# Head norms of a two-block transformer kernel: row sums on four column quarters, factors on 1024 columns, broadcast by ones products on four row quarters

## The chip, the cores and the metric

The kernel runs on 1 core of one Trainium2 chip. The metric is the device time of one execution in microseconds (us). Five engines work side by side: TensorE (PE in the profile, its weight loads PEld), VectorE (DVE), ScalarE (ACT), GpSimd (POOL) and SyncE (SP, which issues the loads of the weights). They meet at semaphores only.

## The reference, cut to what matters

Two blocks follow each other on 256 tokens of width 1024: one with gated linear attention and a feed-forward part, one that adds a gated delta rule (8 heads of 128) and a banded attention, and again a feed-forward part. The change touches three norms of the delta rule. Each takes, for one token and one head, the sum of 128 squares:

```
q = l2norm(q.reshape(b_, s_, A_HEADS, A_DK)) * (A_DK ** -0.5)
k = l2norm(k.reshape(b_, s_, A_HEADS, A_DK))
...
o = chunk_gated_delta_rule(q, k, v, g, beta)
o = o * lax.rsqrt(jnp.mean(jnp.square(o), axis=-1, keepdims=True) + RMS_EPS)
o = o * norm_w.astype(jnp.float32) * jax.nn.silu(z...)
```

So one norm has 8 heads x 256 tokens = 2048 factors.

## The kernel before

Activations lie feature-major: 128 features on the partitions, tokens along the columns. A head of q, k or the delta output is one tile of 128 x 256; eight heads are 128 x 2048. All weights stream from HBM as halves of 128 x 1024 (`raw`, a ring of six), which ACT rounds into `w_hi` (L969) and DVE turns into the remainder `w_lo` (L1478), both in rings of four. TensorE multiplies a panel of two halves in four **quarters**, two to a half, each of 12 matmuls (L401; three passes hi*hi, hi*lo, lo*hi), into four `panel_banks`. The other four PSUM banks, `work_banks` (MB in the code), belong to the delta rule and the attention.

Each engine's order is written by hand. While the delta rule is worked out, TensorE fills its gaps with quarters of the later projections: `fill(step)` multiplies as many as the table FILL says stand behind that step, and `tend(step)` on ACT and DVE prepares the halves for them. FILL places 5 quarters behind `k_sums` and 5 more behind `q_sums`, one behind each of the products, 6 behind `delta_out` (quarters 42 to 47), 8 behind `delta_sums` (48 to 55) and 4 behind `delta_norm` (56 to 59). Quarters 2h and 2h+1 need half h (`open_half` waits for `parts_ready`, that is for DVE's `w_lo`). In `tend("delta_sums")` halves 25, 26 and 27 are prepared, in `tend("delta_norm")` halves 28 to 31.

The norms. Squares of q and k are made on ACT (L1259). `qk_norm` (L715) multiplies them by an all-ones matrix, four matmuls of 128 x 512 over the four work banks: each bank then holds the sums, repeated on all 128 partitions. ACT takes Ln and Exp(-0.5 x) of all 2048 columns into SBUF (k at L1288 and L1290, q at L1293 and L1298), and DVE multiplies keys (L1841), beta times keys (L1843) and queries (L1846). Key sums come first, the query sums follow when ACT has read the first. Then L757 makes six groups of 8 products in the same work banks, two banks at a time, and DVE reads each (L1859) before its banks are written again. The delta output has the same pattern: sums (L852), Ln and Exp in two halves of 1024 columns (L983, L984, called by `factor`), two multiplications on DVE (L1920).

An older place in the program, the gates of the first block, already uses parts of the array: L511 multiplies 128-row operands into 32 columns of the array at a time, L521 32-row operands on four row groups.

Of the kernel before, what the change touches and what calls it, by code (L numbers as in the profile page):

```python
# [17 lines left out]
ALU = mybir.AluOpType  # L18
ACT = mybir.ActivationFunctionType
AX_X = mybir.AxisListType.X  # L20

P = 128
D = 1024
# [59 lines left out]
CONSTANTS, GLA_CONSTANTS, ALL_CONSTANTS = 9, 15, 55  # L83
# [37 lines left out]
def two_blocks(nc, panels, x, ctx_x, columns, c_rows, w_glr, w_gate, w_beta_a, head_rows, rel_bias, out):  # L121
# [3 lines left out]
    with ExitStack() as ctx:  # L125
# [5 lines left out]
        def S(name):  # L131

            if name not in signals:
                signals[name] = ctx.enter_context(nc.semaphore(name))
            return signals[name]
# [108 lines left out]
        with ExitStack() as scope:  # L244
# [7 lines left out]
            rs2 = vb.rearrange("p a b -> p (a b)")  # L252
# [3 lines left out]
            rsq = tt_.rearrange("p a b -> p (a b)")  # L256
# [50 lines left out]
        def _(pool):  # L307
            made = [0]

            def step(ins):  # L310
                made[0] += 1
                ins.then_inc(S("constants"), 1)
                pool.wait_ge(S("constants"), made[0])
# [31 lines left out]
            step(pool.memset(eps[:, 2:3], 1.0))  # L345
            step(pool.memset(wgp, 0.0))
# [26 lines left out]
            pool.wait_ge(S("qk_normed"), 2)  # L373
            pool.memset(tt_[64:P, :, 0:64], 0.0).then_inc(S("corner_cleared"), 1)
# [3 lines left out]
        def _(pe):  # L378
# [333 lines left out]
            def qk_norm(part):  # L712

                for b in range(4):
                    ins = pe.matmul(MB[:, b, :], ones[:, 0:P], sq3[:, part * 8 + 2 * b:part * 8 + 2 * b + 2, :],  # L715
                                    start=True, stop=True)
                ins.then_inc(S("qk_sums"), 1)
# [25 lines left out]
            qk_norm(1)  # L743
            fill("k_sums")
            pe.wait_ge(S("sums_read"), 1)
            qk_norm(0)
            fill("q_sums")

            pe.wait_ge(S("sums_read"), 2)
            pe.wait_ge(S("kb_ready"), 1)  # L750
            for r, (rhs, tj, ti) in enumerate(((kb, 0, 0), (kb, 1, 1), (kb, 0, 1), (qkv, 0, 0), (qkv, 1, 1), (qkv, 0, 1))):
                if r == 3:
                    pe.wait_ge(S("qk_normed"), 2)
                if r >= 2:
                    pe.wait_ge(S("products_read"), r - 1)
                for h in range(DH):
                    ins = pe.matmul(MB[:, 2 * (r % 2) + h // 4, (h % 4) * P:(h % 4) * P + P],  # L757
                                    qkv[:, 8 + h, tj * P:tj * P + P], rhs[:, h, ti * P:ti * P + P], start=True, stop=True)
                ins.then_inc(S("products"), 1)
                fill(("product", r))  # L760
# [88 lines left out]
            for b in range(4):  # L849
                pe.wait_ge(S("delta_squares"), b + 1)  # L850
                pe.wait_ge(S("delta_scaled"), b + 1)
                ins = pe.matmul(MB[:, b, :], ones[:, 0:P], odq[:, 2 * b:2 * b + 2, :], start=True, stop=True)  # L852
                if b % 2:
                    ins.then_inc(S("delta_norm_sum"), 1)
            fill("delta_sums")
            fill("delta_norm")

            pe.wait_ge(S("delta_factor"), 2)
# [79 lines left out]
        def _(act):  # L938
# [42 lines left out]
            def factor(out_, sums, n, which, name):  # L981

                then(act.activation(out_, sums, ACT.Ln, scale=1.0 / n, bias=eps[:, which:which + 1]))  # L983
                act.activation(out_, out_, ACT.Exp, scale=-0.5).then_inc(S(name), 1)  # L984
# [183 lines left out]
            def flat(v):  # L1168
                return v.rearrange("p a b -> p (a b)")
# [116 lines left out]
            all_banks = MB[:].rearrange("p a b -> p (a b)")  # L1286
            act.wait_ge(S("qk_sums"), 1)
            act.activation(rs2, all_banks, ACT.Ln, bias=eps[:, 0:1]).then_inc(S("sums_read"), 1)  # L1288
            act.wait_ge(S("sums_read"), 1)
            act.activation(rs2, rs2, ACT.Exp, scale=-0.5).then_inc(S("qk_factor"), 1)  # L1290
            tend("k_sums")
            act.wait_ge(S("qk_sums"), 2)
            act.activation(rsq, all_banks, ACT.Ln, bias=eps[:, 0:1]).then_inc(S("sums_read"), 1)  # L1293
# [3 lines left out]
            act.wait_ge(S("sums_read"), 2)  # L1297
            act.activation(rsq, rsq, ACT.Exp, scale=-0.5).then_inc(S("qk_factor"), 1)  # L1298
# [37 lines left out]
            for n in range(2):  # L1336
                act.wait_ge(S("delta_norm_sum"), n + 1)
                factor(rs2[:, D * n:D * n + D], flat(MB[:, 2 * n:2 * n + 2, :]), DDK, 0, "delta_factor")
# [123 lines left out]
        def _(dve):  # L1462
# [376 lines left out]
            dve.wait_ge(S("qk_factor"), 1)  # L1839
            kc = qkv[:, 8:16, :]  # L1840
            dve.tensor_tensor(flat(kc), flat(kc), rs2, ALU.mult).then_inc(S("qk_normed"), 1)  # L1841
            dve.wait_ge(S("qk_normed"), 1)
            dve.tensor_tensor(flat(kb), flat(kb), flat(kc), ALU.mult).then_inc(S("kb_ready"), 1)  # L1843
            tend("k_sums")
            dve.wait_ge(S("qk_factor"), 2)
            dve.scalar_tensor_tensor(flat(qkv[:, 0:8, :]), flat(qkv[:, 0:8, :]), DDK ** -0.5, rsq,  # L1846
# [68 lines left out]
            tend("delta_out")  # L1915
            dve.wait_ge(S("delta_scaled"), 4)
            for n in range(2):
                dve.wait_ge(S("delta_factor"), n + 1)
                o = flat(od[:, 4 * n:4 * n + 4, :])
                dve.tensor_tensor(o, o, rs2[:, D * n:D * n + D], ALU.mult).then_inc(S("delta_gated"), 1)  # L1920
            tend("delta_sums")
# [231 lines left out]
```

## Time and profile before

| | us |
|---|---|
| median of 3 runs | 1060.26 |
| the three runs | 1060.14, 1060.26, 1066.72 |
| profiled execution | 1059.05 |
| its span | 1057.3 |
| mean granted TensorE clock | 0.973 of full |

The profile is of one execution, and its span is 1.75 us shorter than that execution's time. A record of a matmul in fp32 comes twice (two records for one instruction of the program). Records of matmuls overlap, since they are pipelined: the spacing of their starts, not their length, is what one costs.

### The profile page before, as it was taken

Reading aid. Unit: us, or ns where it says so; the run is one execution under the profiler, and the core shown is the slowest. Engines: PE = TensorE matmul, PEld = TensorE weight load, DVE = VectorE, ACT = ScalarE, POOL = GpSimd, SP = SyncE. Lnnn points to the kernel's source line nnn. Section 1 sums busy time; section 2 is a strip of 40 time slices with the busy share of each in tenths; the row PEclk is TensorE's granted clock in tenths of the full one; section 3 lists DMA queues with packets and bytes.
Section 4 is the critical chain, followed back from the end, with each engine's and each line's share of the span. In section 5 each row is a group of like instructions: output and inputs, shape, how many; then the busy total and the mean of one; then the engine's idle time right before and its main releaser. Section 6 shows DMA issues by size and latency. Waiting matters only on the chain.

```text
span 1057.3 us, 19933 instructions
## 1 busy us (share of the span) xinstructions
PE 980.9 (93%) x8478; PEld 918.5 (87%) x8478; DVE 703.9 (67%) x1098; ACT 551.0 (52%) x830; POOL 27.2 (3%) x70
## 2 busy tenths in 40 slices
PE   5897999979999999699999999989999699999996
PEld 1477999869999999599898999888898699999995
DVE  2669937547777766598865543555668578888743
ACT  2658431555544443565745342656764466666433
POOL 2010000000000000130100000000000000000000
PEclk9898999999999999899999999999999989999999
DMA  9632765536888888247433436444357525555931
GB/s 329 234 121 80 264 234 187 181 127 212 278 275 283 281 274 309 72 149 252 153 120 102 149 113 169 140 160 132 110 201 228 208 99 184 189 188 188 331 100 40
DMA packets 57113, 196.79 MB, mean 186 GB/s; under 512 B 6064, under 2 KB 10560, under 8 KB 56768
## 3 DMA queue, kind: packets, MB, share of 16 engines
q1 hardware_dynamic: 51552, 187.72, 52.3%
q10 hardware_dynamic: 5216, 7.53, 2.6%
q8 instruction: 67, 1.10, 0.4%
q0 software_dynamic: 256, 0.26, 0.1%
q14 instruction: 22, 0.18, 0.0%
HBM read 194.43 MB, written 1.06 MB: 185 GB/s over the span
## 4 chain that ended last, share of the span: by engine, by line
PE 81%; DVE 9%; ACT 5%; DMA 3%; issue 1%; SPq 0%; ACTq 0%; DVEq 0%
PE panel_banks L401 67%; DMA raw<-in_panels 3%; PE work_banks L786 2%; DVE w_lo L1478 2%; PE work_banks L614 2%; ACT w_hi L969 1%; PE work_banks L573 1%; DVE raw L1511 1%; PE work_banks L715 1%; PE panel_banks L454 1%; PE work_banks L757 1%; PE work_banks L546 1%; PE work_banks L869 1%; PE work_banks L488 1%; PE work_banks L814 1%
## 5 line engine op out<-in xcount | busy, mean ns | idle before, releaser
L401 PE MATMUL panel_banks<-act_hi,w_hi 128*128 128x256 f32 (+1 forms) x1600 | 463.3, 290 | 26.3 <-DVE act_lo L1674 11.4
L401 PE MATMUL panel_banks<-act_lo,w_hi 128*128 128x256 f32 (+1 forms) x1600 | 454.5, 284 | 0.0
L401 PE MATMUL panel_banks<-act_hi,w_lo 128*128 128x256 f32 (+1 forms) x1600 | 453.9, 284 | 0.0
L1478 DVE TENSOR_TENSOR w_lo<-raw,w_hi 128x1024 fp32r<-128x1024 f32 x260 | 315.3, 1222 | 163.5 <-ACT w_hi L969 162.8
L969 ACT ACTIVATE w_hi<-raw 128x1024 fp32r<-128x1024 f32 x260 | 272.0, 1054 | 151.4 <-PE panel_banks L401 130.4
L401 PEld LDWEIGHTS panel_banks<-act_hi,w_hi 128*128 128x128 f32 x1600 | 304.6, 190 | 39.5 <-issue 19.5
L401 PEld LDWEIGHTS panel_banks<-act_lo,w_hi 128*128 128x128 f32 x1600 | 304.7, 190 | 1.8 <-issue 0.5
L401 PEld LDWEIGHTS panel_banks<-act_hi,w_lo 128*128 128x128 f32 x1600 | 304.4, 190 | 1.4
L401 PE MATMUL panel_banks<-hidden_hi,w_hi 128*128 128x256 f32 x352 | 98.0, 278 | 2.3 <-ACT hidden_hi L1186 2.3
L401 PE MATMUL panel_banks<-hidden_hi,w_lo 128*128 128x256 f32 x352 | 97.9, 278 | 0.0
L401 PE MATMUL panel_banks<-hidden_lo,w_hi 128*128 128x256 f32 x352 | 97.7, 278 | 0.0
L1511 DVE CUSTOM_DVE_ANT_0 raw<-raw,c_wide 128x1024 f32<-128x1024 f32 x80 | 94.5, 1220 | 0.4 <-DMA raw<-in_panels 0.3
L401 PEld LDWEIGHTS panel_banks<-hidden_hi,w_hi 128*128 128x128 f32 x352 | 65.9, 187 | 2.9 <-ACT hidden_hi L1186 1.7
L401 PEld LDWEIGHTS panel_banks<-hidden_lo,w_hi 128*128 128x128 f32 x352 | 66.1, 188 | 0.0
L401 PEld LDWEIGHTS panel_banks<-hidden_hi,w_lo 128*128 128x128 f32 x352 | 66.1, 188 | 0.0
L401 PE MATMUL panel_banks<-w_hi,act_hi 128*128 128x256 f32 x192 | 54.5, 284 | 2.2 <-DVE w_lo L1478 2.2
L401 PE MATMUL panel_banks<-w_lo,act_hi 128*128 128x256 f32 x192 | 53.4, 278 | 0.0
L401 PE MATMUL panel_banks<-w_hi,act_lo 128*128 128x256 f32 x192 | 53.4, 278 | 0.0
L2053 DVE SCALAR_TENSOR_TENSOR ffn_work<-panel_banks,columns,ffn_work 128x255 f32<-128x255 f32 (+1 forms) x88 | 38.4, 478 | 21.2 <-ACT ffn_work L1434 20.4
L614 PE MATMUL work_banks<-ffn_work,ones 128*128 128x256 f32 x112 | 31.1, 425 | 14.4 <-ACT ffn_work L1412 4.8
L614 PEld LDWEIGHTS work_banks<-ffn_work,ones 128*128 128x128 f32 x112 | 22.3, 210 | 21.1 <-issue 6.2
L1434 ACT ACTIVATE ffn_work<-panel_banks,columns 128x256 f32<-128x256 f32 x44 | 22.4, 561 | 31.4 <-PE panel_banks L401 31.4
(269 smaller groups left out, 1032.9 us busy)
## 6 DMA issues: line engine op xcount, KB each, us to landing
raw<-in_panels SPq DMA_DIRECT2D x356, 512.0 KB, 5.0
mix_work<-delta_rows ACTq DMA_DIRECT2D x2, 1024.0 KB, 11.8
x_t<-in_x ACTq DMA_DIRECT2D x1, 1024.0 KB, 9.4
gla_work<-in_ctx_x ACTq DMA_DIRECT2D x1, 1024.0 KB, 14.3
mix_work<-in_rel_bias ACTq DMA_DIRECT2D x1, 1024.0 KB, 10.0
out_x<-ffn_work SPq DMA_DIRECT2D x2, 512.0 KB, 2.6
mix_work<-in_rel_bias ACTq DMA_DIRECT2D x1, 768.0 KB, 14.3
c_wide<-in_c_rows ACTq DMA_DIRECT2D x1, 512.0 KB, 16.6
```

The lines of the kernel that those rows point to most:

```text
L401: ins = pe.matmul(out_, a, b, start=start and p == 0, stop=stop and p == 2, skip_group_check=True)
L454: ins = pe.matmul(PB[0:2, a % TURNS, 0:256], cact[:, 0:2, 4 * h + k], raw[:, u % RAW, k * 256:k * 256 + 256], start=(h == 0 and k == 0), s ...
L488: ins = pe.matmul(MB[:, 0, :], ones[:, 0:P], sq1[:, k, :], start=(k == 0), stop=(k == 3))
L546: ins = pe.matmul(MB[:, h, t * T:t * T + T], g_k3[:, 4 * d + h, t * P:t * P + P], g_q3[:, 4 * d + h, :], start=(d == 0), stop=(d == 1))
L573: ins = pe.matmul(MB[:, (h + 2) % 4, v * T:v * T + T], g_v[:, n, h * GDV + v * P:h * GDV + v * P + P], g_a[:, h, n, :], start=(n == 2 and ...
L614: ins = pe.matmul(MB[:, bank, 0:T], ones[:, 0:P], src[:, k, :], start=(k == 0), stop=(k == KT - 1))
L786: ins = pe.matmul(o, lhs[half, m, :], rhs[half, m, :], start=True, stop=True)
L969: act.activation(whi[:, v_ % PARTS, :], raw[:, u % RAW, :], ACT.Copy)\
L1434: ins = act.activation(f_u[:, i % 2, m, :], b[:, m * T:m * T + T], ACT.Identity, scale=col("conv_ffn_2", 88 + 22 * m + i), bias=col("b_con ...
L1478: dve.tensor_tensor(wlo[:, v_ % PARTS, :], raw[:, u % RAW, :], whi[:, v_ % PARTS, :].bitcast(F32), ALU.subtract)\
L1511: dve.tensor_tensor_reduce(raw[:, u % RAW, :], raw[:, u % RAW, :], cwide[:], 1.0, 0.0, ALU.mult, ALU.add, dst).then_inc(S("accumulated"), 1)
L2053: ins = dve.scalar_tensor_tensor(o, b[:, m * T:m * T + T - s], col("conv_ffn_2", 44 * (2 - s) + 22 * m + i), o, ALU.mult, ALU.add)
```

## The change

The ones products are cut into pieces that lie side by side in the array. `group_sums` multiplies the squares of two heads per group by 128 x 32 ones; the four groups write the four partition quarters (32 rows each) of one work bank, so that a bank holds all 2048 sums, each repeated on 32 rows. Keys and queries are summed together, into two banks. ACT takes Ln and Exp of 1024 columns once for both, and of 512 columns for the delta output. `spread` brings the factors back to 128 partitions: 32-row ones times 32-row factors, one row quarter to one work bank, 8 matmuls of 256 columns. The sum over 32 equal rows makes a factor 32, which the scale of 1024 under the root takes out (a fourth column of `eps`, one more memset of 128 x 1 at the start). DVE now multiplies by the work banks instead of by SBUF. On TensorE the spread of the keys stands ahead of `fill("q_sums")`, that of the queries behind it, that of the delta output between `fill("delta_sums")` and `fill("delta_norm")`.

```diff
-            def qk_norm(part):
-                for b in range(4):
-                    ins = pe.matmul(MB[:, b, :], ones[:, 0:P], sq3[:, part * 8 + 2 * b:part * 8 + 2 * b + 2, :],
-                                    start=True, stop=True)
-                ins.then_inc(S("qk_sums"), 1)
+            def group_sums(squares, bank, name):
+                for half in range(2):
+                    for g in range(4):
+                        ins = pe.matmul(MB[32 * g:32 * g + 32, bank, half * T:half * T + T], ones[:, 0:32],
+                                        squares(2 * g + half), start=True, stop=True)
+                        if half:
+                            ins.then_inc(S(name), 1)
+            def spread(factors, name):
+                for half in range(2):
+                    for g in range(4):
+                        rows = slice(32 * g, 32 * g + 32)
+                        ins = pe.matmul(MB[:, g, half * T:half * T + T], ones[rows, 0:P],
+                                        factors[rows, half * T:half * T + T], start=True, stop=True)
+                        if half:
+                            ins.then_inc(S(name), 1)
...
-            qk_norm(1)
+            for part in range(2):
+                group_sums(lambda h: sq3[:, 8 * part + h, :], part, "qk_sums")
             fill("k_sums")
-            pe.wait_ge(S("sums_read"), 1)
-            qk_norm(0)
+            pe.wait_ge(S("qk_factor"), 1)
+            spread(group_rs[:, 512:D], "qk_spread")
             fill("q_sums")
-            pe.wait_ge(S("sums_read"), 2)
+            pe.wait_ge(S("qk_normed"), 1)
+            spread(group_rs[:, 0:512], "qk_spread")
+            pe.wait_ge(S("qk_normed"), 2)
             pe.wait_ge(S("kb_ready"), 1)
...
             fill("delta_out")
-            for b in range(4):
-                pe.wait_ge(S("delta_squares"), b + 1)
-                pe.wait_ge(S("delta_scaled"), b + 1)
-                ins = pe.matmul(MB[:, b, :], ones[:, 0:P], odq[:, 2 * b:2 * b + 2, :], start=True, stop=True)
-                if b % 2:
-                    ins.then_inc(S("delta_norm_sum"), 1)
+            pe.wait_ge(S("delta_squares"), 4)
+            pe.wait_ge(S("delta_scaled"), 4)
+            group_sums(lambda h: odq[:, h, :], 0, "delta_norm_sum")
             fill("delta_sums")
+            pe.wait_ge(S("delta_factor"), 1)
+            spread(group_rs[:, 0:512], "delta_spread")
             fill("delta_norm")
-            pe.wait_ge(S("delta_factor"), 2)
+            pe.wait_ge(S("delta_gated"), 2)
...
-            act.wait_ge(S("qk_sums"), 1)
-            act.activation(rs2, all_banks, ACT.Ln, bias=eps[:, 0:1]).then_inc(S("sums_read"), 1)
-            act.wait_ge(S("sums_read"), 1)
-            act.activation(rs2, rs2, ACT.Exp, scale=-0.5).then_inc(S("qk_factor"), 1)
+            def group_factor(sums, scale, name):
+                o = group_rs[:, 0:sums.shape[1]]
+                then(act.activation(o, sums, ACT.Ln, scale=scale, bias=eps[:, 3:4]))
+                act.activation(o, o, ACT.Exp, scale=-0.5).then_inc(S(name), 1)
+            act.wait_ge(S("qk_sums"), 8)
+            group_factor(flat(MB[:, 0:2, :]), 1024.0, "qk_factor")
             tend("k_sums")
-            act.wait_ge(S("qk_sums"), 2)
-            act.activation(rsq, all_banks, ACT.Ln, bias=eps[:, 0:1]).then_inc(S("sums_read"), 1)
...
-            act.wait_ge(S("sums_read"), 2)
-            act.activation(rsq, rsq, ACT.Exp, scale=-0.5).then_inc(S("qk_factor"), 1)
             tend("q_sums")
...
-            for n in range(2):
-                act.wait_ge(S("delta_norm_sum"), n + 1)
-                factor(rs2[:, D * n:D * n + D], flat(MB[:, 2 * n:2 * n + 2, :]), DDK, 0, "delta_factor")
+            act.wait_ge(S("delta_norm_sum"), 4)
+            group_factor(MB[:, 0, :], 1024.0 / DDK, "delta_factor")
...
-            dve.wait_ge(S("qk_factor"), 1)
+            tend("k_sums")
+            dve.wait_ge(S("qk_spread"), 4)
...
-            tend("k_sums")
-            dve.wait_ge(S("qk_factor"), 2)
+            dve.wait_ge(S("qk_spread"), 8)
...
             tend("delta_out")
+            tend("delta_sums")
             dve.wait_ge(S("delta_scaled"), 4)
+            dve.wait_ge(S("delta_spread"), 4)
             for n in range(2):
-                dve.wait_ge(S("delta_factor"), n + 1)
                 o = flat(od[:, 4 * n:4 * n + 4, :])
-                dve.tensor_tensor(o, o, rs2[:, D * n:D * n + D], ALU.mult).then_inc(S("delta_gated"), 1)
-            tend("delta_sums")
+                dve.tensor_tensor(o, o, flat(MB[:, 2 * n:2 * n + 2, :]), ALU.mult).then_inc(S("delta_gated"), 1)
             tend("delta_norm")
```

The order on DVE around the key and query norms, before (L1837 is the decay difference, L1841, L1843 and L1846 multiply k, beta k and q, `mix_work` is the work area in SBUF):

```order
L1837 TENSOR_TENSOR mix_work<-mix_work,mod_cols 128x8x128 x2
L1841 TENSOR_TENSOR mix_work<-mix_work 128x2048 [waits qk_factor]
L1843 TENSOR_TENSOR mix_work<-mix_work 128x2048 [waits qk_normed]
L1478 TENSOR_TENSOR w_lo<-raw,w_hi 128x1024 [waits upper_ready] x2
L1846 SCALAR_TENSOR_TENSOR mix_work<-mix_work 128x2048 [waits qk_factor]
L1478 TENSOR_TENSOR w_lo<-raw,w_hi 128x1024 [waits upper_ready] x2
L1859 TENSOR_TENSOR mix_work<-work_banks,mix_work 128x1024 [waits products,decay_exp,constants]
```

And now:

```order
L1847 TENSOR_TENSOR mix_work<-mix_work,mod_cols 128x8x128 x2
L1488 TENSOR_TENSOR w_lo<-raw,w_hi 128x1024 [waits upper_ready] x2
L1853 TENSOR_TENSOR mix_work<-mix_work,work_banks 128x2048 [waits qk_spread]
L1855 TENSOR_TENSOR mix_work<-mix_work 128x2048 [waits qk_normed]
L1857 SCALAR_TENSOR_TENSOR mix_work<-mix_work,work_banks 128x2048 [waits qk_spread]
L1488 TENSOR_TENSOR w_lo<-raw,w_hi 128x1024 [waits upper_ready] x2
L1870 TENSOR_TENSOR mix_work<-work_banks,mix_work 128x1024 [waits products,decay_exp,constants]
```

Two preparations of weights have moved ahead of the keys' multiplication, and k and q read the work banks.

The order on DVE around the delta output's norm, before (L1912 and L1923 scale by gain and gate, L1920 and L1932 multiply by the factors, the ISA rows start the banded attention):

```order
L1912 SCALAR_TENSOR_TENSOR mix_work<-work_banks,columns,mix_work 128x512 [waits delta_squares] x3
L1478 TENSOR_TENSOR w_lo<-raw,w_hi 128x1024 [waits upper_ready] x2
L1920 TENSOR_TENSOR mix_work<-mix_work 128x1024 [waits delta_factor,delta_scaled]
L1920 TENSOR_TENSOR mix_work<-mix_work 128x1024 [waits delta_factor]
L1478 TENSOR_TENSOR w_lo<-raw,w_hi 128x1024 [waits upper_ready] x7
L1934 ISA mix_work<-work_banks,mix_work 128x128 [waits band_scores,bias_landed,delta_gated]
```

And now:

```order
L1923 SCALAR_TENSOR_TENSOR mix_work<-work_banks,columns,mix_work 128x512 [waits delta_squares] x3
L1488 TENSOR_TENSOR w_lo<-raw,w_hi 128x1024 [waits upper_ready] x5
L1932 TENSOR_TENSOR mix_work<-mix_work,work_banks 128x1024 [waits delta_spread,delta_scaled]
L1932 TENSOR_TENSOR mix_work<-mix_work,work_banks 128x1024
L1488 TENSOR_TENSOR w_lo<-raw,w_hi 128x1024 [waits upper_ready] x4
L1945 ISA mix_work<-work_banks,mix_work 128x128 [waits band_scores,bias_landed,delta_gated]
```

Three preparations (halves 25 to 27) have moved ahead of the two multiplications; four (halves 28 to 31) still stand behind them.

## Rows read from the trace of the kernel before

**Rows 1.** The page: busy time by engine; a costly group (busy, mean ns).
```profile
PE 980.9 (93%) x8478; PEld 918.5 (87%) x8478; DVE 703.9 (67%) x1098; ACT 551.0 (52%) x830; POOL 27.2 (3%) x70
...
L969 ACT ACTIVATE w_hi<-raw 128x1024 fp32r<-128x1024 f32 x260 | 272.0, 1054 | 151.4 <-PE panel_banks L401 130.4
```
**Rows 2.** Chain of waits, 514 to 560 us: start us, us, what.
```profile
516.32 5.39 PE work_banks L715 x8
521.71 6.80 PE panel_banks L401 x60
528.52 3.43 PE work_banks L715 x8
531.95 4.25 PE panel_banks L401 x36
```
**Rows 3.** TensorE in order of time, 534 to 566 us: start us, us, what [idle before].
```profile
538.85 3.73 PE L757 MATMUL work_banks<-mix_work 128*128 128x128 f32 x32
...
544.20 2.05 PE L757 MATMUL work_banks<-mix_work 128*128 128x128 f32 x16 [0.20 <-DVE mix_work L1859]
```
**Rows 4.** ScalarE in order of time, key factors.
```profile
523.04 1.98 ACT L1288 ACTIVATE mix_work<-work_banks,eps 128x2048 f32<-128x2048 f32 x1
```
**Rows 5.** VectorE in order of time, query norm and next.
```profile
538.45 2.29 DVE L1846 SCALAR_TENSOR_TENSOR mix_work<-mix_work 128x2048 f32<-128x2048 f32 x1 [4.26 <-ACT mix_work L1298]
540.66 2.36 DVE L1478 TENSOR_TENSOR w_lo<-raw,w_hi 128x1024 fp32r<-128x1024 f32 x2
```
**Rows 6.** TensorE in order of time, the first block's gates (parts of the array).
```profile
65.09 1.95 PE L511 MATMUL work_banks<-gla_work 128*32 128x128 f32 x64
...
74.11 0.40 PE L401 MATMUL panel_banks<-act_hi,w_lo 128*128 128x512 f32 x1
74.44 1.17 PE L521 MATMUL work_banks<-gla_work 32*128 32x128 f32 x32
...
75.89 0.39 PE L401 MATMUL panel_banks<-act_lo,w_hi 128*128 128x512 f32 x1
```
**Rows 7.** Chain of waits, 655 to 685 us.
```profile
658.46 1.73 PE work_banks L852 x4
...
660.21 1.12 ACT mix_work L983
...
664.55 1.23 DVE mix_work L1920
665.77 1.15 DVE w_lo L1478
...
666.96 13.88 PE panel_banks L401 x120
```
**Rows 8.** One line's instructions (L1334), duration ns min/median/max.
```profile
L1334 ACT ACTIVATE mix_work<-work_banks x4: 592/602/621, 648.7 to 650.1; 128x512 f32<-128x512 f32 x4
```
**Rows 9.** TensorE in order of time, first work behind four idle stretches [idle before].
```profile
428.24 4.04 PE L614 MATMUL work_banks<-ffn_work,ones 128*128 128x256 f32 x13 [2.39 <-ACT ffn_work L1213]
...
516.32 5.39 PE L715 MATMUL work_banks<-mix_work,ones 128*128 128x512 f32 x8 [1.97 <-ACT mix_work L1259]
...
697.25 0.55 PE L401 MATMUL panel_banks<-act_hi,w_hi 128*128 128x256 f32 x1 [2.94 <-DVE w_lo L1478]
...
837.09 1.15 PE L614 MATMUL work_banks<-ffn_work,ones 128*128 128x256 f32 x2 [2.82 <-ACT ffn_work L1412]
```
**Rows 10.** Windows, TensorE: length, PE busy (records), granted clock, DMA share, GB/s.
```profile
64.00:77.00 13.00, 12.42 (x164) 1.00 0.35 118
428.30:431.30 3.00, 2.89 (x11) 1.00 0.73 229
516.30:519.70 3.40, 3.38 (x4) 0.51 0.46 147
...
697.30:700.70 3.40, 3.40 (x16) 0.50 0.63 188
...
837.10:840.50 3.40, 3.40 (x8) 0.52 0.47 174
```

More of the change, by code:

```diff
@@ L80 @@
     NCOL += _n
-CONSTANTS, GLA_CONSTANTS, ALL_CONSTANTS = 9, 15, 55
+CONSTANTS, GLA_CONSTANTS, ALL_CONSTANTS = 10, 16, 56
 N_SPLIT = sum(count * pattern.count("S") for _, pattern, count in LAYERS)
@@ L251, in two_blocks @@
             vb = take(2, D)
-            rs2 = vb.rearrange("p a b -> p (a b)")
+            group_rs = vb.rearrange("p a b -> p (a b)")[:, 0:D]
             dm = take(DH, 384)
@@ L255, in two_blocks @@
             tt_ = take(16, P)
-            rsq = tt_.rearrange("p a b -> p (a b)")
             t_at = take.at[0]
@@ L345, in _ @@
             step(pool.memset(eps[:, 2:3], 1.0))
+            step(pool.memset(eps[:, 3:4], 1024 * EPS_RMS))
             step(pool.memset(wgp, 0.0))
@@ L373, in _ @@
             pool.wait_ge(S("qk_normed"), 2)
+            pool.wait_ge(S("decay_masked"), 2)
             pool.memset(tt_[64:P, :, 0:64], 0.0).then_inc(S("corner_cleared"), 1)
@@ L742, in _ @@
             pe.wait_ge(S("tok_ready"), 1)
-            qk_norm(1)
+            for part in range(2):
+                group_sums(lambda h: sq3[:, 8 * part + h, :], part, "qk_sums")
             fill("k_sums")
-            pe.wait_ge(S("sums_read"), 1)
-            qk_norm(0)
+            pe.wait_ge(S("qk_factor"), 1)
+            spread(group_rs[:, 512:D], "qk_spread")
             fill("q_sums")
-            pe.wait_ge(S("sums_read"), 2)
+            pe.wait_ge(S("qk_normed"), 1)
+            spread(group_rs[:, 0:512], "qk_spread")
+            pe.wait_ge(S("qk_normed"), 2)
             pe.wait_ge(S("kb_ready"), 1)
             for r, (rhs, tj, ti) in enumerate(((kb, 0, 0), (kb, 1, 1), (kb, 0, 1), (qkv, 0, 0), (qkv, 1, 1), (qkv, 0, 1))):
-                if r == 3:
-                    pe.wait_ge(S("qk_normed"), 2)
                 if r >= 2:
@@ L1285, in _ @@
             exp_table()
-            all_banks = MB[:].rearrange("p a b -> p (a b)")
-            act.wait_ge(S("qk_sums"), 1)
-            act.activation(rs2, all_banks, ACT.Ln, bias=eps[:, 0:1]).then_inc(S("sums_read"), 1)
-            act.wait_ge(S("sums_read"), 1)
-            act.activation(rs2, rs2, ACT.Exp, scale=-0.5).then_inc(S("qk_factor"), 1)
+            def group_factor(sums, scale, name):
[4 more added lines that the diff above has]
+            group_factor(flat(MB[:, 0:2, :]), 1024.0, "qk_factor")
             tend("k_sums")
-            act.wait_ge(S("qk_sums"), 2)
-            act.activation(rsq, all_banks, ACT.Ln, bias=eps[:, 0:1]).then_inc(S("sums_read"), 1)
             act.wait_ge(S("decay_diff"), 3)
@@ L1838, in _ @@
                                   over_tokens(gl_tok[:, row, tj, :], P), op).then_inc(S("decay_diff"), 1)
-            dve.wait_ge(S("qk_factor"), 1)
+            all_banks = MB[:].rearrange("p a b -> p (a b)")
+            tend("k_sums")
+            dve.wait_ge(S("qk_spread"), 4)
             kc = qkv[:, 8:16, :]
-            dve.tensor_tensor(flat(kc), flat(kc), rs2, ALU.mult).then_inc(S("qk_normed"), 1)
+            dve.tensor_tensor(flat(kc), flat(kc), all_banks, ALU.mult).then_inc(S("qk_normed"), 1)
             dve.wait_ge(S("qk_normed"), 1)
             dve.tensor_tensor(flat(kb), flat(kb), flat(kc), ALU.mult).then_inc(S("kb_ready"), 1)
-            tend("k_sums")
-            dve.wait_ge(S("qk_factor"), 2)
-            dve.scalar_tensor_tensor(flat(qkv[:, 0:8, :]), flat(qkv[:, 0:8, :]), DDK ** -0.5, rsq,
+            dve.wait_ge(S("qk_spread"), 8)
+            dve.scalar_tensor_tensor(flat(qkv[:, 0:8, :]), flat(qkv[:, 0:8, :]), DDK ** -0.5, all_banks,
                                      ALU.mult, ALU.mult).then_inc(S("qk_normed"), 1)
```

## The prediction

> **What bounds the kernel now.** I read the page first: TensorE is busy 93% of the span [rows 1], so time is saved by giving it less work or fewer waits, and an instruction taken from ACT or DVE counts only where TensorE waits for it. Then the chain of waits over the two stretches that the change touches. In the first [rows 2, 3] nearly everything is TensorE: key sums 5.39 us, 60 matmuls of fill 6.80, query sums 3.43, and fill again from 531.95 until the products start at 538.85. These add up to the whole stretch from 516.32, so TensorE never waits in it. The long factors on ACT (1.98 us for Ln of the keys [rows 4]) are hidden behind fill. The first trace of them is the 0.20 us that TensorE waits at 544.20 [rows 3]: DVE's query multiplication ended late (540.7), and behind it stood two `w_lo` (2.36 us) and the read of the first product [rows 5]. In the second stretch [rows 7] the factors are on the chain: ACT from 660.21, DVE's multiplication at 664.55, a `w_lo` at 665.77, and only then, at 666.96, does TensorE go on with quarter 50. It had finished quarter 49 at about 664.65 (below), so it stood still for 2.3 us. After that 120 matmuls without a gap (13.88 us, 0.1157 each) bring it to the banded attention at 680.85.
>
> The clock: in the stretch behind 516.32 the key sums ran at half the granted clock, 0.51 over 3.4 us [rows 10], that is mostly at 1.2 GHz instead of 2.4, after TensorE had waited 1.97 us [rows 9]. That is why 8 records took 5.39 us there and 3.43 us for the queries [rows 2].
>
> **The parts, costed.** *Sums on column quarters.* Nearest rows: L511, 64 records of 128 columns on 32-column parts, 1.95 us [rows 6]. Keys and queries together are now 16 instructions, 32 records of 256 columns, the same number of columns in all, so 1.95 us at the full clock; I take 2.0. If the quarters did not overlap they would cost 16 x 0.43 = 6.86 us (one 512-column instruction is 3.43/4 = 0.86). For the delta output half of it, and I take 1.05.
>
> *Spread on row quarters.* Nearest rows: L521, 32 records of 128 columns, 1.17 us [rows 6]; the new spread has 16 records of 256 columns, the same columns. Its floor is a quarter of the serial 3.43, 0.86 us. Its ceiling is what L521 took from its neighbours: the matmul before starts at 74.11 and streams 0.23 (512 columns, twice 0.1157), to 74.34; the second one behind starts at 75.89, so the first had begun in effect at 75.66: 1.32 us. I take 1.1, near the middle, as there are half as many instructions.
>
> Those rows also show the price of entering parts of the array: 74.34 to 74.44, 0.10 us. The Trainium skill ("TensorEngine Tiling (Array Packing)", section Key Properties) says that a change of tiling mode drains TensorE, a rule that speaks against this change, which makes ten such changes. The rows agree in kind; at 0.10 us each it would be 1.0 us, and my 2.0, 1.1 and 1.05 hold most of it.
>
> *First stretch.* The clock falls behind 516.32 as before, since nothing ahead of it changes: 3.4 us at about half speed do 1.7 us of the 2.0, so the sums take 3.7 us, 1.7 less than 5.39. Then fill 6.80, spread of the keys 1.1, fill 6.90 (531.95 to 538.85), spread of the queries 1.1: 19.6 us instead of 22.5, and TensorE is there at 535.9. Are the factors in time? ACT starts at 523.04 as before (it was held up by other work, not by the sums), and Ln of 1024 columns takes 1.12 us [rows 7], Exp as much, so it is done at 525.3; the keys' spread at 526.8 need not wait. DVE does two `w_lo` first (to about 528.8), then keys and beta keys (2.3 us each, as the queries' [rows 5]) to 533.4; the queries' spread at 534.8 need not wait either. But here is the new wait: the product groups write the work banks that DVE reads as query factors, so TensorE must wait for the query multiplication, and that can start only at 535.9. It takes 2.29 us [rows 5], and from PSUM hardly more: the read of the first product, 1024 columns, filled 543.0 to 544.2 [rows 3, 5], 1.2 us, twice that is 2.4. Products start at 538.3, 0.6 earlier than now. The 0.20 us at 544.20 goes too, because ACT has the next `w_hi` ready and DVE reads the first product at 540.6 to 541.8, before TensorE needs the bank at 543.4. **First stretch: 0.8 us gained**, with a fresh idle stretch of 2.4 us in it.
>
> *Second stretch.* Sums began at 658.46 [rows 7], so TensorE was through them at 661.9 and through quarters 48 and 49 (24 x 0.1157 = 2.8) at 664.65. Now: sums to 659.5. ACT: Ln and Exp of 512 columns, 0.6 us each [rows 8], to 660.75; `w_hi` 1.05 [rows 1] to 661.8; DVE's `w_lo`, no longer behind two multiplications, 1.2 to 663.0. TensorE finishes quarter 49 at 662.3, waits 0.8, and does quarters 50 to 55 (72 matmuls, 8.3 us) to 671.4, spread to 672.5. Halves 28 to 31, though, stand on DVE behind the two multiplications, and these behind the spread. In the rows one multiplication and one `w_lo` took 664.55 to 666.96, 2.4 us [rows 7]; with the second multiplication it is 3.6. TensorE stands until 676.1, then 48 matmuls (5.55): 681.6 instead of 680.85. **Second stretch: 0.8 us lost.** The 3 us that ACT saves pay for the old wait, and the new one is longer.
>
> *The clock.* Idle stretches of 2.94 and 2.82 us were followed by 3.4 us at 0.50 and 0.52; one of 1.97 too; one of 2.39 was not (1.00) [rows 9, 10], nor was the 2.3 before 666.96, as the 0.1157 behind it shows. So the new 3.6 us wait very likely brings a fall, and 3.4 us at half speed cost 1.7 us. The 2.4 us wait lies among the uncertain ones, two without and one with; I take none. Quartered blocks themselves kept 1.00 in 64 to 77 us [rows 10].
>
> *Nothing else counts.* The memset at the start ends long before TensorE's first ones product. The memset behind `qk_normed` on POOL had its second wait fulfilled already. The loads of weights are issued when `w_lo` is done, earlier in the first stretch, later for halves 28 on; what they bring (halves 34 on) is needed only behind the 8 quarters of the step `scores` (96 x 0.1157 = 11 us), and that is the cover here.
>
> Sum: -0.8 + 0.8 + 1.7 = +1.7 us. On the profiled execution's 1059.05 that gives 1060.75, on the median (1060.26, which is 1.2 us above the profiled one) 1061.96. I predict the middle, **1061.4 us**.
>
> **The rivals.** *The short wait also drops the clock* (2.4 us at 535.9). Against it, two of the three rows near it; for it, 1.97 us sufficed once. +3.4 us: 1063.1 by the same middle base (1059.7). *Neither drops it*: the base, 1059.7; or the wait at 672 is shorter than I think. *The saving comes through whole*: TensorE saves 2.9 us of work in the first stretch, 1.3 in the second, and the 2.3 us wait: -6.5, 1053.2. It would need DVE to read query factors while products are written, and the wait in the code forbids it. *The quarters do not overlap*, the case on the slow side: 256-column pieces with weights loaded for each might queue one behind the other, where 128-column ones in L511 overlapped. Then the first stretch has sums of 3.4 + (6.86 - 1.7) = 8.6 us, +3.2; two spreads of 3.43 for one query sum, +3.4; the wait of 2.4, less the 0.2: +8.8. The second has equal sums, a wait of 0.7 in place of 2.3 (-1.6), spread +3.4, wait +3.6: +5.4, and the clock +1.7. Together +15.9, 1075.6. It passes 1% when two thirds of the overlap are lost. L511 (1.95 us for what would be 6.86) speaks against it.
>
> The Trainium skill ("TensorE: Matmul & The Clock Gate", section The cost: per-tile semaphore tail) says that increments of several tiles are serialised, about 26 ns each; the change has four behind each block where one would do. By it an estimated 0.08 us comes on top of each of five blocks, 0.4 us; no row here separates it.
>
> **The numbers.** My forecast 0.45; both waits drop the clock 0.2; neither 0.15; whole saving 0.03; no overlap 0.03; 0.14 for a changed clock at one of the later idle stretches (such as those of 2.94 and 2.82 us), 1.7 us up or down. The range: below, no fall, blocks at their floors (-0.8) and one later fall gone (-1.7) from 1059.05, 1056.5; above, both falls (+3.4), ceilings (+1.0) and most of one more fall (+1.4) on 1060.26, 1066. A difference of 1% (10.6 us) is about what can be told from no change here. Only the missing overlap passes it on the slow side, 0.03; on the fast side 0.01 is left; the rest, 0.96, is the same.
>
> **What would show it.** Sums near 516 of 3.7 us and spreads of 1.1; an idle stretch of 2.4 us before the first product group, ended by DVE's query multiplication; ACT's Ln and Exp at 1.1 and 0.6 us; an idle 0.8 us before quarter 50 and 3.6 before quarter 56, ended by `w_lo`; a granted clock of 0.5 for 3.4 us behind the latter. I am wrong if records of a block are spaced as serial ones, if reading PSUM makes DVE's 2048 columns much longer than 2.3 us, or if ACT reaches the key factors after 526.8.

## The result, and the profile after

The changed kernel takes 1069.57 us (median of 20 runs, 1064.52 to 1074.3), the kernel before 1065.48 (20 runs beside them, 1060.14 to 1068.73). The ratio is 1.0048, with a 95% interval of 1.0032 to 1.0064: 5.1 us longer (3.4 to 6.8), inside 1%; the two medians lie 4.1 us apart. Every difference of times below is the ratio's, on 1065 us. The profiled execution took 1069.25 us, with a span of 1067.5 and a mean granted clock of 0.965; that of before had 1059.05, 1057.3 and 0.973.

The page after, busy time by engine, as [rows 1]:

```profile
PE 986.0 (92%) x8550; PEld 928.0 (87%) x8550; DVE 704.2 (66%) x1098; ACT 543.2 (51%) x826; POOL 26.9 (3%) x71
```

ACT has the 8 us less that the shorter factors promised. TensorE has 5.1 us more, although its products take less time at equal clock: the mean granted clock is lower, 0.965 against 0.973, so more of its work was done at half speed.

The chain of waits after, 510 to 565 us (start, length, what), as [rows 2, 3]:

```profile
521.47 3.41 PE work_banks L717 x32
524.88 7.42 PE panel_banks L402 x60
532.30 1.07 PE work_banks L727 x16
533.37 7.26 PE panel_banks L402 x60
540.64 1.20 PE work_banks L727 x16
...
541.86 2.30 DVE mix_work L1857
...
544.20 5.47 PE work_banks L770 x32
```

L717 is the sums on column quarters, L727 the spread on row quarters, L402 the fill, L770 the product groups. The sums of 32 records take 3.41 us where 16 took 5.39 + 3.43, each spread 1.07 to 1.20. And between the last spread and the first product group TensorE waits for the query multiplication, L1857. VectorE in order of time in the same place:

```profile
534.73 2.28 DVE L1853 TENSOR_TENSOR mix_work<-mix_work,work_banks 128x2048 f32<-128x2048 f32 x1
...
541.86 2.29 DVE L1857 SCALAR_TENSOR_TENSOR mix_work<-mix_work,work_banks 128x2048 f32<-128x2048 f32 x1 [2.53 <-PE work_banks L727]
```

And ScalarE:

```profile
528.20 1.12 ACT L1301 ACTIVATE mix_work<-work_banks,eps 128x1024 f32<-128x1024 f32 x1
```

ACT's 1.98 us of [rows 4] is 1.12. DVE itself waits 2.53 us for the spread, then TensorE waits for DVE: each in turn. The second stretch, chain of waits 655 to 700 us, as [rows 7]:

```profile
665.19 1.12 PE work_banks L717 x16
...
666.34 0.70 ACT mix_work L1301
...
667.60 1.05 ACT w_hi L981
...
668.67 1.24 DVE w_lo L1488
...
669.95 8.74 PE panel_banks L402 x72
678.70 1.20 PE work_banks L727 x16
...
679.99 2.35 DVE mix_work L1932 x2
682.34 1.15 DVE w_lo L1488
...
683.62 8.23 PE panel_banks L402 x48
```

The wait before quarter 50 has shrunk from 2.3 us to 0.82, and a new one stands before quarter 56: two multiplications (L1932, 2.35 us) and one `w_lo`. The 48 matmuls behind it take 8.23 us, where e5 below has 5.65 without a wait. TensorE in order of time, first work behind the three waits [idle before]:

```profile
544.20 2.06 PE L770 MATMUL work_banks<-mix_work 128*128 128x128 f32 x14 [2.49 <-DVE mix_work L1857]
...
669.95 0.38 PE L402 MATMUL panel_banks<-w_hi,act_hi 128*128 128x256 f32 x1 [0.82 <-DVE w_lo L1488]
...
683.62 0.55 PE L402 MATMUL panel_banks<-w_hi,act_hi 128*128 128x256 f32 x1 [3.85 <-DVE w_lo L1488]
```

Windows (length, PE, PEld, DVE, ACT, POOL busy, granted clock, DMA share, GB/s), as [rows 10]:

```profile
545.30:549.20 3.90, 3.90 (x23) 3.90 (x22) 2.34 (x2) 0.00 (x0) 0.00 (x0) 0.56 0.68 220
682.40:683.60 1.20, 0.00 (x0) 0.01 (x1) 1.20 (x2) 0.00 (x0) 0.00 (x0) 0.50 0.00 0
683.60:689.20 5.60, 5.58 (x27) 5.60 (x28) 3.29 (x3) 0.00 (x0) 0.00 (x0) 0.52 0.69 206
689.20:691.80 2.60, 2.60 (x26) 2.47 (x24) 0.00 (x0) 0.00 (x0) 0.00 (x0) 1.00 0.66 227
```

Behind both longer waits TensorE worked near 1.2 GHz, the lower of its two levels: 3.9 us at 0.56 and 5.6 us at 0.52, then 1.00 again.

**The two profiles can't be subtracted.** The span is 10.2 us longer, but the sums start at 521.47 against 516.32 [rows 2], so 5.15 us lie ahead of the first changed product. One window of before, and the same stretch of time in after:

```profile
439.00:452.00 13.00, 11.90 (x82) 9.38 (x83) 10.71 (x23) 5.38 (x11) 6.92 (x21) 0.78 0.12 43
```

```profile
439.00:452.00 13.00, 8.04 (x41) 7.48 (x42) 11.60 (x25) 4.30 (x9) 2.86 (x8) 0.61 0.00 0
```

Ahead of the sums the two programs differ by one small memset, and yet after is behind here, and its granted clock is 0.61 where before has 0.78. Ahead of the sums the half clock was granted for 34 us before and for 41 us after, which at half speed is 3.4 of the 5.15 us; where the rest comes from is not shown. In the traces below the start of the sums falls anywhere from 519.75 to 524.51 us, and at 521.17 in e7, which has the old norms. So the start scatters from execution to execution, whatever the norms are, and below I compare two stretches of the trace: **A**, from the start of the sums to the first solve product behind the product groups, and **B**, from the start of the delta sums to the first product of the banded attention. Before, A is 46.8 us and B 22.5. After, A is 48.3 and B 26.7, together 5.7 more. What lies between A and B is 95.1 to 95.4 us in every trace.

### The profile page after: what moved, and what is told of

Same layout as the page of the kernel before. It is cut to its first block, busy times and chain, and to the rows that moved or that the text cites. A ratio compares the mean times of both kernels' runs of the same rounds, so it can differ in the third digit from the quotient of the medians.

```text
span 1067.5 us, 20071 instructions
## 1 busy us (share of the span) xinstructions
PE 986.0 (92%) x8550; PEld 928.0 (87%) x8550; DVE 704.2 (66%) x1098; ACT 543.2 (51%) x826; POOL 26.9 (3%) x71
## 4 chain that ended last, share of the span: by engine, by line
PE 83%; DVE 9%; ACT 4%; DMA 2%; issue 1%; SPq 0%; ACTq 0%; DVEq 0%
PE panel_banks L402 68%; PE work_banks L615 2%; DMA raw<-in_panels 2%; DVE w_lo L1488 2%; PE work_banks L799 2%; PE work_banks L770 1%; PE work_banks L574 1%; DVE raw L1521 1%; ACT w_hi L981 1%; PE work_banks L547 1%; PE work_banks L881 1%; PE panel_banks L455 1%; PE work_banks L827 1%; PE work_banks L489 0%; DVE x_t L1721 0%
## 5 line engine op out<-in xcount | busy, mean ns | idle before, releaser
L402 PE MATMUL panel_banks<-act_hi,w_hi 128*128 128x256 f32 (+1 forms) x1600 | 464.3, 290 | 25.6 <-DVE act_lo L1684 10.6
L402 PE MATMUL panel_banks<-act_lo,w_hi 128*128 128x256 f32 (+1 forms) x1600 | 455.6, 285 | 0.0
L402 PE MATMUL panel_banks<-act_hi,w_lo 128*128 128x256 f32 (+1 forms) x1600 | 455.3, 285 | 0.0
L402 PEld LDWEIGHTS panel_banks<-act_hi,w_hi 128*128 128x128 f32 x1600 | 305.4, 191 | 39.8 <-issue 20.1
L402 PEld LDWEIGHTS panel_banks<-act_lo,w_hi 128*128 128x128 f32 x1600 | 305.7, 191 | 1.5
L402 PEld LDWEIGHTS panel_banks<-act_hi,w_lo 128*128 128x128 f32 x1600 | 305.5, 191 | 1.6
L402 PE MATMUL panel_banks<-hidden_hi,w_hi 128*128 128x256 f32 x352 | 98.7, 280 | 2.3 <-ACT hidden_hi L1198 2.3
L402 PE MATMUL panel_banks<-hidden_lo,w_hi 128*128 128x256 f32 x352 | 98.4, 280 | 0.0
L402 PE MATMUL panel_banks<-hidden_hi,w_lo 128*128 128x256 f32 x352 | 98.2, 279 | 0.0
L402 PEld LDWEIGHTS panel_banks<-hidden_hi,w_hi 128*128 128x128 f32 x352 | 66.1, 188 | 2.9 <-ACT hidden_hi L1198 1.7
L402 PEld LDWEIGHTS panel_banks<-hidden_hi,w_lo 128*128 128x128 f32 x352 | 66.0, 188 | 0.0
L402 PEld LDWEIGHTS panel_banks<-hidden_lo,w_hi 128*128 128x128 f32 x352 | 66.0, 187 | 0.0
L402 PE MATMUL panel_banks<-w_hi,act_hi 128*128 128x256 f32 x192 | 55.6, 290 | 4.7 <-DVE w_lo L1488 4.7
L402 PE MATMUL panel_banks<-w_lo,act_hi 128*128 128x256 f32 x192 | 54.6, 284 | 0.0
L402 PE MATMUL panel_banks<-w_hi,act_lo 128*128 128x256 f32 x192 | 54.6, 284 | 0.0
L402 PEld LDWEIGHTS panel_banks<-w_hi,act_hi 128*128 128x128 f32 x192 | 37.4, 195 | 6.0 <-issue 5.0
```

What stands on the lines that cost most here:

```text
L402: ins = pe.matmul(out_, a, b, start=start and p == 0, stop=stop and p == 2, skip_group_check=True)
```

## The experiments

Two theories. **W**: the whole loss is the two new waits, which DVE's order makes, and the low clock that follows them. **Q**: the products on parts of the array cost more than their rows show, for themselves or for their neighbours. Times are medians, ratios to the kernel before on the same chip with 95% intervals; different kernels are compared by these ratios. An interval is about 2 us to either side, so a difference of two such ratios is uncertain by about 3 us, and the stretches A and B of the traces have to carry the finer readings.

**e1, e2: one half of the change alone.** e1 has the old delta norm again, against the changed kernel:

```diff
-            group_sums(lambda h: odq[:, h, :], 0, "delta_norm_sum")
+            for b in range(4):
+                ins = pe.matmul(MB[:, b, :], ones[:, 0:P], odq[:, 2 * b:2 * b + 2, :], start=True, stop=True)
...
```

e2 has the old key and query norms:

```diff
-            for part in range(2):
-                group_sums(lambda h: sq3[:, 8 * part + h, :], part, "qk_sums")
+            qk_norm(1)
...
```

> The change for keys and queries alone; the delta output's norm is as before. Theory W (the loss is the two new waits and the low clock behind them): 2.95 us less work on TensorE, a wait of 2.4 to 2.5 us before the products, and a fall of the clock behind it in some executions, 0 to 1.7 us: between 0.6 faster and 1.1 slower than before. Theory Q (products on parts of the array cost more than their rows show, or slow their neighbours): three of the five blocks stand here, so about three fifths of the 5 us, 3 us slower.

> The change for the delta output alone; keys and queries are as before. Theory W: 1.3 us less work, waits of 0.8 and 3.85 in place of 2.3, and low clock for one to two stretches of 3.4 us, 1.7 to 2.7 us: 2.7 to 4 us slower than before. Theory Q: two of the five blocks, about 2 us slower.

Measured: e1 1065.18 us, 1.0007 (0.9984 to 1.0029), +0.7 us. e2 1066.64, 1.0031 (1.0011 to 1.0052), +3.3. The delta norm has the larger share of the loss, though the two intervals overlap. The three blocks of e1 have together 64 records on parts of the array; that they cost nothing speaks against Q only weakly, since its 3 us stand just inside the interval. e1's A is 48.3 us (the clock fell behind its wait) and its B 24.1, because there the old wait, 2.34 us long, was followed by a fall too; e2's B is 25.7.

**e3, e4, e5: the waits taken away.** e3 lets DVE do the two halves that are waited for ahead of the delta multiplications. e4 spreads the query factors after 8 quarters of fill instead of 10, so that DVE's multiplication runs beside the last two. e5 does both. The edit of e3, on DVE, and that of e4, on TensorE:

```diff
             tend("delta_sums")
+            for _ in range(2):
+                lower_half(2 * j + taken[0] + PARTS)
+                taken[0] += 1
             dve.wait_ge(S("delta_scaled"), 4)
```

```diff
-            fill("q_sums")
+            fill("q_sums", 8)
             pe.wait_ge(S("qk_normed"), 1)
             spread(group_rs[:, 0:512], "qk_spread")
+            fill("q_sums")
             pe.wait_ge(S("qk_normed"), 2)
```

> The changed kernel with halves 28 and 29 prepared by VectorE ahead of the delta output's two multiplications instead of behind them; TensorE's order is untouched. Theory W: no wait before quarter 56 and no fall of the clock there, 3.85 + 1.7 to 2.7 = 5.5 to 6.5 us faster than the changed kernel, so 0.4 to 1.4 faster than before. Theory Q: the wait alone goes, 3.85 us, and with the blocks' cost left the kernel stays 1.2 us slower than before.

> The changed kernel with the spread of the query factors after quarter 7 instead of after quarter 9, so that VectorE multiplies the queries while TensorE does two more quarters. Theory W: the wait of 2.5 us before the products goes, and with it the fall of the clock that the profiled execution had there, 2.5 to 4.2 us faster than the changed kernel, 1 to 2.5 slower than before. Theory Q: 2.5 us faster than the changed kernel.

> Both moves at once: query factors spread after quarter 7, halves 28 and 29 ahead of the delta output's multiplications. Theory W: both new waits and the low clock behind them are gone; TensorE keeps 2.95 us of saved work in the first stretch and 3.6 us (1.3 of work, 2.3 of wait replaced by 0.8) in the second: 4 to 6 us faster than before. The two single moves measured 1.9 faster and 1.6 slower than before, 7.0 and 3.5 us better than the changed kernel's 5.1 slower: their sum gives 5.4 faster. Theory Q: blocks cost more than their rows, the gain over before is under 2 us.

Measured: e3 1062.33 us, 0.9982 (0.9960 to 1.0004), 1.9 less than before and 7.0 less than the changed kernel. e4 1065.69, 1.0015 (0.9997 to 1.0033), +1.6. e5 1058.86 (6 runs), 0.9934 (0.9913 to 0.9956): **7.0 us less than before** (4.7 to 9.3), where the single moves add up to 5.4 and W gave 4 to 6. In the traces each move takes the loss out of its own stretch alone: e3 has B at 19.9 with A still at 48.3, e4 has A at 44.1 with B still at 25.2. Chains of waits of e5, first stretch and second:

```profile
522.07 3.61 PE work_banks L717 x32
525.67 7.26 PE panel_banks L402 x60
532.93 1.08 PE work_banks L727 x16
534.01 4.44 PE panel_banks L402 x36
538.45 1.07 PE work_banks L727 x16
539.53 3.02 PE panel_banks L402 x24
542.55 3.57 PE work_banks L771 x32
```

```profile
666.34 8.45 PE panel_banks L402 x72
674.78 1.08 PE work_banks L727 x16
675.86 5.65 PE panel_banks L402 x48
681.51 0.86 PE work_banks L882 x8
```

No engine but TensorE in the first, and no wait between 666.34 and 681.51 in the second: the product groups follow the fill at once, and the 32 of them take 3.57 us instead of 5.47, the 48 matmuls 5.65 instead of 8.23. A is 44.1 us (4.1 less than after), B 19.9 (6.7 less).

**e6: the blocks doubled.** e5 with every spread done twice over, the same results written again:

```diff
-                for half in range(2):
+                for half in (0, 1, 0, 1):
```

> As the kernel with both moves, but each spread multiplies everything twice (the second time over the first, same result): 16 products instead of 8, three times. Theory W: each block costs what its row says, 1.1 us, all three stand on TensorE's path: 2.6 (streaming floor, 3 x 0.86) to 3.3 us slower than the kernel with both moves. Theory Q: clearly over 4 us slower.

Measured: 1060.61 us, 0.9953 (0.9927 to 0.9979), 2.0 more than e5, a difference too small for these intervals to tell from 0 or from 4. The trace decides. Its chain of waits:

```profile
530.60 1.94 PE work_banks L729 x32
532.54 4.44 PE panel_banks L402 x36
536.98 1.94 PE work_banks L729 x32
```

32 records take 1.94 us, 16 took 1.07: 16 more cost 0.87, a quarter of the serial 3.43 [rows 2] to within 0.01. What a block costs beside that is 0.20 us, for entering and for its four increments. Three doubled blocks are 2.6 us in the rows; Q wanted over 4. By the rows Q has fallen.

**e7: the old norms, with one half moved.** In the kernel before, the old wait of 2.3 us is taken away in the same manner, by an edit on ACT and one on DVE:

```diff
             tend("delta_out")
+            upper_half(2 * j + taken[0] + PARTS)
             for n in range(2):
```

```diff
             tend("delta_out")
+            lower_half(2 * j + taken[0] + PARTS)
             dve.wait_ge(S("delta_scaled"), 4)
```

> The kernel before with one edit: half 25 is prepared ahead of the delta factors on ScalarE and ahead of the two multiplications on VectorE. The wait of 2.3 us before quarter 50 goes, without any product on a part of the array. Theory W: 2 to 2.3 us faster than before, if half 26, which still stands behind the factors, comes in time for quarter 52 (needed at 667.4, ready by about 669 at worst: then only 0.7 faster). Theory Q says the same; this run tells how much of the second stretch's gain needed the new form at all.

Measured: 1062.8 us, 0.9974 (0.9955 to 0.9992), 2.8 less than before, B 20.1. Its chain of waits:

```profile
663.51 3.43 PE work_banks L852 x8
666.95 16.61 PE panel_banks L401 x144
```

144 matmuls without a gap. So the delta norm's part of what the change could bring was to be had without it, by the trace: B 20.1 with the old norm, 19.9 to 20.0 with the new one and the halves moved.

**e8: the wait filled with useless work.** The changed kernel, with 28 products ahead of quarter 56, into the bank that this quarter overwrites (`fill` no longer takes a bank of its own for it). The wait stays, TensorE is busy in it:

```diff
             spread(group_rs[:, 0:512], "delta_spread")
+            held[:] = [take_turn()]
+            for n in range(28):
+                pe.matmul(PB[:, held[0], 0:T], hhi[:, n % KT, 0:P], hhi[:, n % KT, :], start=True, stop=True)
             fill("delta_norm")
```

> The changed kernel with 28 products of 128x256, of no use, in the long wait before quarter 56; they write a bank that quarter 56 then overwrites. VectorE's path to quarter 56 is as long as before, so the wait on it stays, but TensorE is busy in most of it. Theory W: the clock stays at its upper level, and the kernel is 1.7 to 2.7 us faster than the changed one, 2.4 to 3.4 slower than before. If the low clock were not part of the price: no difference from the changed kernel (5 slower than before).

Measured: 1065.46 us, 1.0009 (0.9988 to 1.0029), 4.1 less than the changed kernel. Chain of waits and window:

```profile
682.67 2.35 DVE mix_work L1935 x2
685.02 1.14 DVE w_lo L1491
...
686.21 5.92 PE panel_banks L402 x48
```

```profile
680.00:692.00 12.00, 11.79 (x105) 11.04 (x103) 6.89 (x6) 1.54 (x2) 0.00 (x0) 1.00 0.32 99
```

DVE is as late as after (2.35 and 1.14 us on the chain), but the granted clock stays at 1.00 (2.4 GHz), and 48 matmuls take 5.92 us instead of 8.23: 2.3 us for the clock alone. B is 24.0 instead of 26.7; the other 0.4 us of that lie ahead of the products (72 matmuls in 8.45 for 8.74, and 0.1 us behind the `w_lo`). The 4.1 us by time are more than the 1.7 to 2.7 expected, and uncertain by 3. This kernel does nothing but keep TensorE from idling, and gets more than half of the 4.2 us back that B had lost in after; against e10, whose fall was shorter (B 25.7, below), its B is 1.8 less.

**e9: one more step on e5.** The query sums while ACT still squares the keys, and a half moved ahead of the delta factors:

```diff
-            pe.wait_ge(S("qk_squares"), 2)
             for part in range(2):
+                pe.wait_ge(S("qk_squares"), part + 1)
...
+            upper_half(2 * j + taken[0] + PARTS)
             act.wait_ge(S("delta_norm_sum"), 4)
```

> The kernel with both moves and two more: TensorE sums the queries' squares while ScalarE still squares the keys (it waits for each part apart, queries first), and ScalarE prepares half 25 ahead of the delta factors. Theory W: of the wait of 2 us ahead of the sums, one product block of 1 us is now inside, so 1 us of work leaves the path and the idle stretches become short (about 1 us in two pieces), so the fall of the clock behind them (3.4 us at half speed, 1.7 us) should go as well; the wait of 0.8 us before quarter 50 goes. Together 1.8 us without the clock and 3.5 with it faster than the kernel with both moves, so 9 to 10.5 faster than before. Theory Q has nothing to say on the waits: 1 to 2 us faster at most.

Measured: 1058.3 us, 0.9953 (0.9935 to 0.9971), 5.0 less than before: not to be told from e5, where 9 to 10.5 less than before was expected, so the expectation failed. Its window 520 to 530 us, and its spreads and first products in order of time [idle before]:

```profile
520.00:530.00 10.00, 9.03 (x91) 7.79 (x92) 7.62 (x11) 7.73 (x10) 0.84 (x1) 1.00 0.42 134
```

```profile
530.93 1.15 PE L727 MATMUL work_banks<-mix_work,ones 32*128 32x256 f32 x16 [0.65 <-ACT mix_work L1303]
...
537.54 1.15 PE L727 MATMUL work_banks<-mix_work,ones 32*128 32x256 f32 x16 [1.02 <-DVE mix_work L1855]
```

The low clock at the sums is gone (1.00), B is 18.8, 1.1 less than in e5. But TensorE, now earlier, waits again, for ACT and for DVE, whose own chain from the squares on is not shortened. Measured from the last product ahead of the sums, this stretch is 50.26 us after, 46.11 in e5 and 45.96 in e9: what the clock gave, the waits took.

**e10: the changed kernel again.**

> The changed kernel itself, once more, on the same chip as the improved one: 5 us slower than before as in its first 20 runs (3.4 to 6.8), and in its trace the waits of 2.5 us before the products and 3.85 us before quarter 56. Theory W: the clock falls behind the second wait in any execution, behind the first in most. Theory Q: the blocks cost the same in every execution.

Measured: 1066.97 us, 1.0039 (1.0017 to 1.0062), +4.2. TensorE in order of time, and windows:

```profile
544.66 2.61 PE L770 MATMUL work_banks<-mix_work 128*128 128x128 f32 x21 [2.49 <-DVE mix_work L1857]
```

```profile
544.70:548.70 4.00, 4.00 (x36) 4.00 (x37) 3.54 (x4) 0.00 (x0) 0.91 (x1) 1.00 0.43 123
683.50:687.00 3.50, 3.50 (x21) 3.50 (x21) 2.20 (x2) 0.00 (x0) 0.00 (x0) 0.59 0.84 273
```

The same wait of 2.49 us to the hundredth, and no fall behind it this time; the fall behind the wait of 3.85 us is there, and shorter. A is 46.4, B 25.7: 2.9 more than before, where the first trace had 5.7.

## Why the prediction was wrong

Forecast 1061.4 us, range to 1066, effect +1.7; measured 1069.57. Of the 8.2 us, 5.8 are the base and 2.4 the effect (by the two medians, +4.1; by the ratio +5.1). Two terms of the sum failed: the base, and the price of the clock behind the two new waits.

**The base** was the middle between the profiled execution and a median of three runs, 1059.7. Twenty runs, the three among them, gave 1065.48. Three runs, two of them 0.12 us apart at 1060.2 and one at 1066.72, had shown the spread, and I took the two for the level. The range's upper end even started from 1060.26. A part of its cause is in the traces: the half clock ahead of the sums, of which the profile of before had drawn the least, 34 us where the other eleven traces have 37 to 48. That is 2 to 7 us of time; why it varies is not shown. This term belonged into the range, on the high side alone, with the 6 us of the third run.

**Sums and spreads: right.** 3.41 us for the sums behind the low clock (3.7 said), 1.12 for the delta's (1.05), spreads of 1.07 to 1.20 (1.1). The quarters overlap: 3.43 against 1.07 to 1.20 is 2.9 to 3.2 times. The Trainium skill ("TensorE: Matmul & The Clock Gate", section Measured speedup vs the span model) gives 3.07 times for four row tiles, and these rows agree. The serial increments of the Trainium skill (the same page, section The cost: per-tile semaphore tail), priced in the prediction at an estimated 0.4 us, 0.08 a block, have room within the 0.20 us that e6 leaves a block, and are not told from entering there.

**The waits: right, place by place.** 2.49 us before the products ended by the query multiplication (2.4 said), 0.82 before quarter 50 (0.8), 3.85 before quarter 56 ended by `w_lo` (3.6). DVE reads 2048 columns from PSUM in 2.28 us, no longer than from SBUF (2.29 [rows 5]). e3, e4 and e5 show that these two waits, with the clock behind them, account for the whole loss: with both gone the kernel is faster than before.

**The parts' sum, slightly off.** Without a fall A was forecast 0.8 shorter and is 0.4 shorter (e10). B was forecast 0.8 longer and is 1.5 longer (e8, clock 1.00; its own useless products no longer hold anything up). In B of e8 the 0.7 too little is mostly fill: 48 matmuls take 5.92 us (5.55 said) and 72 take 8.45 (8.3 said; 8.74 after); the spread is 1.20 (1.1). In A the fill of 60 takes 7.26 us in e5, where the old form had 6.80 and 6.90. I had priced fill at 0.1157 a matmul throughout, from one stretch of 120. Whether the blocks ahead of it make it slower is not shown, for in the kernel before 72 matmuls behind products on the whole array (L835) also took longer than the 8.33 of this price:

```profile
649.97 8.48 PE panel_banks L401 x72
```

**The clock: the step of the effect that failed.** "The 2.4 us wait lies among the uncertain ones, two without and one with; I take none." The changed form's wait there was followed by a fall in four of the five traces that have it (after, e1, e3, e8; not e10). A fall costs 1.9 us (A 48.3 against 46.4). The row nearest in length, and without a fall, was itself the exception. Ahead of L614 TensorE waited 2.39 us at 428.24, and the clock stayed at 1.00 [rows 9, 10]. The same wait, of 2.37 to 2.39 us, stands in all twelve traces, and in the other eleven the clock fell behind it. In after, TensorE in order of time and a window (as [rows 10]):

```profile
432.46 1.93 PE L615 MATMUL work_banks<-ffn_work,ones 128*128 128x256 f32 x5 [2.38 <-ACT ffn_work L1225]
...
433.00:436.40 3.40, 3.40 (x10) 2.50 (x9) 0.28 (x1) 3.40 (x10) 0.00 (x0) 0.50 0.85 277
```

One profile had shown me one draw for each wait, and I read it as a rule. And behind the wait of 3.85 us I took 3.4 us at half speed, 1.7; e10 had that, while in after the half clock held until 689, 5.6 us of work at 0.52, which is 2.7 us (the 48 matmuls alone: 8.23 against 5.92 in e8, 2.3). With the falls as they came, -0.4 + 1.5 for the parts, 1.9 for four in five of the short wait (1.5) and 1.8 to 2.7 for the long one: +4.4 to +5.3, and +4.2 and +5.1 were measured. The rival that had both waits drop the clock was the right mechanism, at a chance of 0.2, and with its 3.4 us for two falls still too cheap.

The direction held, slower, and so did the bound: a difference under 1%, given 0.96.

**Open:** why the same 2.49 us wait is followed by a fall in one trace and not in another, and why the fall behind 3.85 us lasts 3.4 us in e2, e4 and e10 and 6.8 after; and why the half clock ahead of the sums varies from execution to execution. No experiment here told that.

## What to carry to other kernels

Work taken from a bound engine is worth what the next engine's order lets through: here 2.9 and 1.3 us of products gone turned into waits for DVE, until two instructions were moved ahead of the multiplications, and a spread two quarters earlier (-7.0 us instead of +5.1). Price an idle stretch of TensorE of 2.3 us or more with the half speed behind it, as likely rather than uncertain, and do not take one trace's row as the rule for it. And take the base from all the runs with their spread, not from the profiled one.

## What the runs showed of the hardware

Idle stretches of TensorE and the clock behind them, from 538 to 720 us: of 0.82 us, none fell; of 1.81, at the first solve product, none in twelve; of 2.25 (before), no fall; of 2.34 (e1, at the old wait), a fall; of 2.49, four falls in five; of 2.94, the wait of [rows 9] at 697.25, which all twelve traces have, eleven falls, and none in e5, whose window behind it shows 1.00:

```profile
697.90:701.90 4.00, 3.98 (x33) 3.48 (x34) 3.96 (x7) 4.00 (x13) 0.00 (x0) 1.00 0.65 180
```

Of 3.85 us, four falls in four where TensorE stood idle (after, e2, e4, e10), none where it was given useless work (e8). Counted from 428 us to the end over all twelve traces, idle stretches of 2.33 to 2.94 us were followed by a fall in 40 of 44 cases. Below that the place matters more than the length: of 1.96 to 2.12 us ahead of the sums, nine falls in nine; of 1.98 to 2.03 between 816 and 828 us, three in ten; of 1.93 from 1045 us on, none in twelve. So the length alone does not decide, and one trace is one draw. In the trace after, the half clock was already granted at 682.4, 1.2 us before the work began.
